# Output projection of a decoder trunk on one core: two of four column groups token-major, turned by one transpose and a trip through memory

## The chip, the cores and the metric

The kernel runs on one core of one Trainium2 chip. The metric is the device time of one execution in microseconds (us); the kernel before was run three times. The profile is of one further execution.

## The reference, cut to what matters

Two layers follow each other. The first mixes tokens (attention and retention), adds its output projection to the residual x, and runs a gated MLP; the second mixes by pooling and runs another MLP. The change lies in the output projection of the first layer and in the normalized copy of x that the MLP behind it reads:

```
def rms_norm(x, g):
    y = xf * lax.rsqrt(jnp.mean(xf * xf, axis=-1, keepdims=True) + EPS)
    return (y * g).astype(x.dtype)

# parallel_mixer: mixed is (1, 256 tokens, 2048), w_out is (2048, 2048)
    mixed = jnp.concatenate([a_out, r_out], axis=-1)
    return jnp.einsum('bse,ed->bsd', mixed, w_out)

# reference, layer 0
    x = x + parallel_mixer(...)
    h = rms_norm(x, ffn_norm[l])
    x = x + conv_ffn(h, w_up[l], conv_w[l], conv_b[l], w_down[l])
```

## The kernel before

Everything is feature-major: x is 128 partitions (features) by 16 feature tiles by S = 256 tokens. A matrix product in float32 is made of three products of rounded parts: a weight w is split in hi (rounded copy, ScalarE, L741) and lo = w - hi (VectorE, L1115), and so is the activation (first and second S columns of h, mixed and act). Products hi*hi, hi*lo and lo*hi are summed in PSUM.

Weights arrive in units of 512 x 512 (1 MB), one DMA each (L315, on SP's queue), in four slots of raw. A unit has four k-tiles (kt) of 128 rows. For each kt ScalarE writes hi[kt] as soon as TensorE has used that kt of the unit before (w_hi waits on w_used), VectorE writes lo[kt], and TensorE waits on lo_done. SP loads unit n when lo of unit n - 4 is made.

TensorE has two ways to use a unit. wide_unit (L385 to L408) keeps the weights stationary: for each kt four products hi x 512 columns (both parts of the activation, L391) and four lo x 256 columns (L395), into four PSUM banks, feature-major. token_unit (L489 to L503) keeps the activation stationary and streams the weights: for each kt six products of 512 columns (L498, L500, L501), into two banks, token-major. The down projections of both MLPs use token_unit for three of their four column groups; there VectorE turns the result with 16 transposes of 32 x 256 (turn_down, L1431) and adds it to x (add_turned).

The output projection is the stage of this case: 16 units, n = 0 to 15, four column groups of four units (n // 4). Groups alternate between banks 4 to 7 and 0 to 3. Before, all four are wide. When group g is summed, VectorE adds both halves of its banks to x in two instructions (add_mixed, L1291 and L1293), right behind its lo of unit n = 4, 8, 12. ScalarE then makes the first part of h (h_spread, L747) between its hi at n = 5, 9, 13 and one square of the group (square, L776) behind it; VectorE makes the second part of h between its lo at n = 6, 10, 14 (h_lo_group, L1150) and adds squares at n = 11, 15 (add_squares, L1125). The last group is handled inside the first units of the up projection. TensorE waits before group g for the evacuation of what the same banks held.

All orders are written out by hand; each engine's instructions run in that order, DMA issues on its own queue among them. ScalarE's queue carried few DMAs before: the gains, a strip of bias written to memory (L886) and read back (L890), and two parts of the output.

Of the kernel before, what the change touches and what calls it, by code (L numbers as in the profile page):

```python
# [23 lines left out]
ALU = mybir.AluOpType  # L24
ACT = mybir.ActivationFunctionType
AX = mybir.AxisListType
F32 = mybir.dt.float32
F32R = mybir.dt.float32r

P = 128  # L30
# [4 lines left out]
KT = 4  # L35

def trunk_kernel(nc, xT, rel_bias, norm_g, w_in, w_out, lam, subln, pool_w, pool_scale,
                 w_up, conv, w_down, bucket_onehot, rot_cos, rot_sin, decay, pool_matrix, ident_in, flip_in, outT):
    D, S = xT.shape  # L40
# [33 lines left out]
    U_OUT = U_IN + NG_IN * 4  # L74
# [6 lines left out]
    G_OUT = len(ACCS) + 1  # L81
# [26 lines left out]
    RET_START = (39, 42, 47, 49)  # L108

    scratch = nc.dram_tensor("bias_strip", (BD, SPAN), F32, kind="Internal").ap()

    TURN = 32
# [3 lines left out]
    with ctx:  # L117
# [5 lines left out]
        x = sb("x", [P, DT, S])  # L123
# [17 lines left out]
        with mixer:  # L141
            qb = [sb(f"q{i}", [P, 4, S], stack=mixer) for i in range(2)]
# [4 lines left out]
            mixed = sb("mixed", [P, DT, 2 * S], F32R, stack=mixer)  # L147
# [33 lines left out]
        ps = ctx.enter_context(nc.psum_tensor("ps", [P, 8, 512], F32))  # L181

        def sem(name):
            return ctx.enter_context(nc.semaphore(name))
# [10 lines left out]
        w_used = sem("w_used")  # L195
        evacuated = sem("evacuated")
# [40 lines left out]
        mix_hi = sem("mix_hi")  # L237
        mix_lo = sem("mix_lo")
        x_half = sem("x_half")
        x_turned = sem("x_turned")  # L240
        half_in = sem("half_in")
        half_sum = sem("half_sum")
# [19 lines left out]
        rstd_copied = sem("rstd_copied")  # L262
        out_ready = sem("out_ready")
        out_done = sem("out_done")

        rstd_b = rstd[:, 0:S]
        rstd_2 = rstd_b.unsqueeze(1).to_broadcast([P, 2, S])
# [26 lines left out]
        def wide_bank(G):  # L294

            return 4 - 4 * (G % 2)
# [83 lines left out]
        def _(pe):  # L380
            def wide_unit(n, base, bank, first, last, moving, ready=None, in_rows=None):

                for kt in range(KT):

                    pe.wait_ge(lo_done, base + KT * n + kt + 1)  # L385
                    if ready is not None:
                        ready(kt)
                    mv = moving(kt)

                    def wide(m):  # L390
                        pe.matmul(ps[:, bank + m, :], hi[:, kt, m * P:(m + 1) * P], mv, start=first and kt == 0,  # L391
                                  stop=False, skip_group_check=True)

                    def narrow(m):
                        return pe.matmul(ps[:, bank + m, S:2 * S], lo[:, kt, m * P:(m + 1) * P], mv[:, 0:S],  # L395
                                         start=False, stop=last and kt == KT - 1, skip_group_check=True)
                    if in_rows is None or kt in in_rows:
                        for row in (0, 2):
                            wide(row)
                            wide(row + 1)  # L400
                            narrow(row)
                            mm = narrow(row + 1)
                    else:
                        for m in range(4):
                            wide(m)
                            mm = narrow(m)
                    mm.then_inc(w_used, 1)

            def opening(j):

                return (0, 3) if j == 0 else ()
# [203 lines left out]
            for n in range(U_OUT):  # L615
                G, j = divmod(n, 4)
                if n in ACC_AT:
                    i = ACC_AT[n]
# [28 lines left out]
            for g in range(4):  # L647
                G = G_OUT + g
                pe.wait_ge(evacuated, G - 1)
                if g == 0:  # L650
                    pe.wait_ge(head_kept, 16)
                    pe.wait_ge(ssq_kept, 8)
                for j in range(4):
                    def mixed_tile(kt, j=j):
                        pe.wait_ge(mix_lo, (KT * j + kt) // 2 + 1)
                    wide_unit(U_OUT + 4 * g + j, 0, wide_bank(G), j == 0, j == 3, lambda kt: mixed[:, KT * j + kt, :],
                              mixed_tile if g == 0 else None, opening(j) if g else None)

            for l in range(DEPTH):
                if l == 1:  # L660
# [54 lines left out]
                for g in range(DN_GROUPS):  # L715
                    G = G_DN[l] + g
                    pe.wait_ge(evacuated, G - 1)
                    for j in range(DN_UNITS):
                        n, whole = U_DN[l] + DN_UNITS * g + j, j == DN_UNITS - 1
# [11 lines left out]
        def _(sc_e):  # L731
# [94 lines left out]
            def mixed_hi(n):  # L826
                sc_e.wait_ge(mix_f32, 2 * (n + 1))
                a_.activation(mixed[:, 2 * n:2 * n + 2, 0:S], mt[:, :, :], ACT.Copy).then_inc(mix_hi, 1)
# [74 lines left out]
                    head_root(6, 8)  # L903
            for n in range(16):
                g = n // 4 - 1
                spread = n >= 4 and n % 4 == 1
                w_hi(U_OUT + n, 0, n % 4, 16 * (R_OUT[0] + n // 4 + 1),
                     h_spread(g, 1, G_OUT + g + 1) if spread else None)
                if n == 0:
                    first_half_in(len(ACCS) - 1)  # L910
                    mixed_hi(4)
                    ret_gate(1)
                if n == 1:
                    mixed_hi(5)
                if n == 2:
                    mixed_hi(6)
                    mixed_hi(7)
                if spread:
                    square(1, g)

# [25 lines left out]
            for l in range(DEPTH):  # L946
# [105 lines left out]
                q = (l + 1) * 2 * PAIRS - 1  # L1052
# [15 lines left out]
                for g in range(1, DN_GROUPS):  # L1068
                    for j in range(DN_UNITS):
                        s = j % 4  # L1070
# [17 lines left out]
            for m in range(4):  # L1088
                t = 12 + m
# [20 lines left out]
        def _(ve):  # L1110
            def w_lo(n, base, slot, kts=range(KT), between=None):

                for kt in kts:
                    ve.wait_ge(hi_done, base + KT * n + kt + 1)
                    ve.tensor_tensor(lo[:, kt, :], raw[:, slot, kt, :], hi[:, kt, :].bitcast(F32),  # L1115
                                     ALU.subtract).then_inc(lo_done, 1)
                    if between is not None:
                        between(kt)

            def add_squares(n, g):  # L1120

                ve.wait_ge(sq_ready, 4 * n + g + 1)
                if g > 1:
                    ve.wait_ge(sq_added, SQ_BASE[n] + g - 1)
                ve.tensor_tensor(sqacc[:, :, :], sqacc[:, :, :], sqt[:, :, :], ALU.add).then_inc(sq_added, 1)  # L1125
# [20 lines left out]
            def h_lo_group(n, g, gain, ms=range(4)):  # L1146
                for m in ms:
                    t = 4 * g + m
                    ve.wait_ge(h_hi, H_BASE[n] + t + 1)
                    ve.scalar_tensor_tensor(h[:, t, S:2 * S], x[:, t, :], gains[:, gain, t:t + 1],  # L1150
                                            h[:, t, 0:S].bitcast(F32), ALU.mult, ALU.subtract).then_inc(h_lo, 1)
# [126 lines left out]
            def decay_scores(r):  # L1278
# [5 lines left out]
                ve.tensor_tensor(sc[:, 0, 0:S], ps[:, 4, 0:S], dec[:, r, :], ALU.mult).then_inc(decayed, 1)  # L1284
                ve.tensor_tensor(sc[:, 0, S:S + P], ps[:, 4, S:S + P], dec[:, r, 0:P], ALU.mult).then_inc(decayed, 1)

            def add_mixed(g):

                ve.wait_ge(w_used, KT * (U_OUT + 4 * (g + 1)))
                b, xs = wide_bank(G_OUT + g), x[:, 4 * g:4 * g + 4, :]  # L1290
                ve.tensor_tensor(xs, ps[:, b:b + 4, 0:S], xs, ALU.add).then_inc(x_half, 1)  # L1291
                ve.wait_ge(x_half, g + 1)
                ve.tensor_tensor(xs, ps[:, b:b + 4, S:2 * S], xs, ALU.add).then_inc(evacuated, 1)  # L1293

            ve.memset(ones[:, :], 1.0).then_inc(setup, 1)
# [66 lines left out]
                    norm_ret(7)  # L1362
            for n in range(16):
                g = n // 4 - 1
                spread = n >= 4 and n % 4 == 2
                w_lo(U_OUT + n, 0, n % 4, between=(lambda kt: h_lo_group(1, g, 1, [kt])) if spread else None)
                if g >= 1 and n % 4 == 3:
                    add_squares(1, g)
                if n == 0:
                    take_out(len(ACCS) - 1)  # L1370
                    mixed_lo(4)
                    mix_ret(5)
                if n == 1:
                    mixed_lo(5)
                    mix_ret(6)
                if n == 2:
                    mixed_lo(6)
                    mix_ret(7)
                    mixed_lo(7)
                if n >= 4 and n % 4 == 0:  # L1380
                    add_mixed(n // 4 - 1)

            def up_add(q, Gp):

# [54 lines left out]
            def add_down(l, g):  # L1439

                ve.wait_ge(w_used, KT * (U_DN[l] + DN_UNITS * (g + 1)))
                b, xs = wide_bank(G_DN[l] + g), x[:, 4 * g:4 * g + 4, :]
                ve.tensor_tensor(xs, ps[:, b:b + 4, 0:S], xs, ALU.add).then_inc(x_half, 1)
                ve.wait_ge(x_half, 4 + l + 1)
                ve.tensor_tensor(xs, ps[:, b:b + 4, S:2 * S], xs, ALU.add).then_inc(evacuated, 1)

            for l in range(DEPTH):
# [118 lines left out]
            for m in range(4):  # L1566
                b, xs = wide_bank(G_DN[1] + 3) + m, x[:, 12 + m, :]
                ve.wait_ge(tail_mm, m + 1)
                ve.tensor_tensor(xs, ps[:, b, 0:S], xs, ALU.add).then_inc(x_half, 1)
                ve.wait_ge(x_half, 5 + m + 1)  # L1570
                ve.tensor_tensor(xs, ps[:, b, S:2 * S], xs, ALU.add).then_inc(last_added, 1)
            ve.wait_ge(token_rms, 1)
            ve.reciprocal(rms[:, 2:4], rms[:, 0:2]).then_inc(token_rstd, 1)
# [124 lines left out]
```

## Time and profile before

| what | value |
|---|---|
| time, median of 3 runs | 1942.24 us (1942.01 to 1942.35) |
| time of the profiled execution | 1942.34 us |
| its span in the profile | 1940.2 us |
| TensorE busy | 1924.7 us, 99% |
| VectorE busy | 1428.8 us, 74% |
| ScalarE busy | 1111.5 us, 57% |
| DMA, mean | 188 GB/s |

The profile's span begins with the first instruction and ends with the last; 2.1 us of the execution lie around it. TensorE's matmuls are pipelined, so the distance from one start to the next says what one costs, not its duration.

### The profile page before, as it was taken

The numbers are of one execution on the slowest core, as the hardware profiler recorded it, in microseconds if no ns is written. First come the engines' busy times: TensorE is split into PE (matmuls) and PEld (weight loads), VectorE is DVE, ScalarE is ACT, GpSimd is POOL, SyncE is SP. The second block draws the span as 40 slices with busy tenths as digits, with TensorE's granted clock in tenths as the row PEclk, the third lists the DMA queues.
The fourth block names the chain that finished last, engine by engine and source line by source line (L and its number), as shares of the span: only waits on it lengthen the run. The fifth ranks groups of instructions, "written<-read, shape, count | busy, mean of one in ns | idle before, by whom it ended". The sixth has DMA issues, their size and how long they took to land.

```text
span 1940.2 us, 30192 instructions
## 1 busy us (share of the span) xinstructions
PE 1924.7 (99%) x10550; PEld 1665.1 (86%) x10550; DVE 1428.8 (74%) x2242; ACT 1111.5 (57%) x1845; POOL 48.7 (3%) x53
## 2 busy tenths in 40 slices
PE   8999999999999999999999999999999999999998
PEld 8888888888888888888888888888888888888887
DVE  6667786767877777777666667877777777756665
ACT  6555544656565656666544556656665566655544
POOL 0002250000000000000000000000000000000000
PEclk9999999999999999999999999999999999999999
DMA  9655555555555555555555555555555555555653
GB/s 327 196 172 160 183 164 169 190 184 190 195 183 187 193 192 182 188 194 168 200 203 191 193 173 177 192 193 183 188 194 191 182 189 195 190 170 191 214 191 108
DMA packets 205203, 364.93 MB, mean 188 GB/s; under 512 B 6563, under 2 KB 49100, under 8 KB 205132
## 3 DMA queue, kind: packets, MB, share of 16 engines
q1 hardware_dynamic: 203388, 362.34, 56.2%
q10 hardware_dynamic: 1744, 1.63, 0.3%
q8 instruction: 47, 0.77, 0.2%
q14 instruction: 24, 0.20, 0.0%
HBM read 361.83 MB, written 2.11 MB: 188 GB/s over the span
## 4 chain that ended last, share of the span: by engine, by line
PE 98%; DVE 1%; ACT 0%; DMA 0%; issue 0%; DVEq 0%; SPq 0%
PE ps L391 41%; PE ps L395 20%; PE ps L498 8%; PE ps L500 8%; PE ps L501 8%; PE ps L464 7%; PE ps L468 3%; PE ps L482 0%; PE ps L484 0%; PE ps L485 0%; DVE ssq L1245 0%; DVE lo L1115 0%; PE ps L670 0%; PE ps L672 0%; PE ps L530 0%; PE ps L583 0%
## 5 line engine op out<-in xcount | busy, mean ns | idle before, releaser
L741 ACT ACTIVATE hi<-raw 128x512 fp32r<-128x512 f32 x1352 | 844.4, 630 | 792.7 <-PE ps L395 470.0
L1115 DVE TENSOR_TENSOR lo<-raw,hi 128x512 fp32r<-128x512 f32 x1360 | 927.9, 697 | 465.1 <-ACT hi L741 459.1
L391 PE MATMUL ps<-h,hi 128*128 128x512 f32 x2816 | 958.2, 394 | 0.0
L395 PE MATMUL ps<-h,lo 128*128 128x256 f32 x2816 | 734.3, 277 | 0.0
L391 PEld LDWEIGHTS ps<-h,hi 128*128 128x128 f32 x2816 | 508.2, 188 | 98.1 <-DVE lo L1115 0.2
L395 PEld LDWEIGHTS ps<-h,lo 128*128 128x128 f32 x2816 | 529.2, 188 | 25.4
L498 PE MATMUL ps<-hi,act 128*128 128x512 f32 x528 | 205.6, 389 | 0.0
L500 PE MATMUL ps<-lo,act 128*128 128x512 f32 x528 | 205.6, 389 | 0.0
L501 PE MATMUL ps<-hi,act 128*128 128x512 f32 x528 | 205.5, 389 | 0.0
L464 PE MATMUL ps<-h,hi 128*128 128x512 f32 x576 | 183.3, 400 | 0.0
L468 PEld LDWEIGHTS ps<-h,lo 128*128 128x128 f32 x576 | 108.3, 188 | 25.4
L498 PEld LDWEIGHTS ps<-hi,act 128*128 128x128 f32 x528 | 99.1, 188 | 20.6
L501 PEld LDWEIGHTS ps<-hi,act 128*128 128x128 f32 x528 | 99.1, 188 | 20.6
L500 PEld LDWEIGHTS ps<-lo,act 128*128 128x128 f32 x528 | 99.1, 188 | 20.4
L391 PE MATMUL ps<-act,hi 128*128 128x512 f32 x336 | 116.0, 394 | 0.0
L468 PE MATMUL ps<-h,lo 128*128 128x256 f32 x576 | 113.4, 278 | 0.0
L395 PE MATMUL ps<-act,lo 128*128 128x256 f32 x336 | 91.9, 277 | 0.0
L464 PEld LDWEIGHTS ps<-h,hi 128*128 128x128 f32 x576 | 88.3, 189 | 0.5
L391 PE MATMUL ps<-mixed,hi 128*128 128x512 f32 x256 | 86.0, 395 | 0.5 <-DVE lo L1115 0.5
L391 PEld LDWEIGHTS ps<-act,hi 128*128 128x128 f32 x336 | 62.6, 188 | 14.0
L395 PE MATMUL ps<-mixed,lo 128*128 128x256 f32 x256 | 63.9, 278 | 0.0
L395 PEld LDWEIGHTS ps<-act,lo 128*128 128x128 f32 x336 | 63.1, 188 | 0.7
(191 smaller groups left out, 1493.8 us busy)
## 6 DMA issues: line engine op xcount, KB each, us to landing
raw<-in_w_up SPq DMA_DIRECT2D x176, 1024.0 KB, 5.0
raw<-in_w_down SPq DMA_DIRECT2D x88, 1024.0 KB, 5.0
raw<-in_w_in SPq DMA_DIRECT2D x54, 1024.0 KB, 5.1
raw<-in_w_out SPq DMA_DIRECT2D x16, 1024.0 KB, 5.1
raw<-in_pool_w SPq DMA_DIRECT2D x4, 1024.0 KB, 5.2
raw<-in_w_in SPq DMA_DIRECT2D x8, 256.0 KB, 4.9
x<-in_xT SPq DMA_DIRECT2D x8, 128.0 KB, 4.7
x<-in_xT SPq DMA_DIRECT2D x2, 512.0 KB, 7.8
```

The source lines that it names most:

```text
L391: pe.matmul(ps[:, bank + m, :], hi[:, kt, m * P:(m + 1) * P], mv, start=first and kt == 0, stop=False, skip_group_check=True)
L395: return pe.matmul(ps[:, bank + m, S:2 * S], lo[:, kt, m * P:(m + 1) * P], mv[:, 0:S], start=False, stop=last and kt == KT - 1, skip_group ...
L464: pe.matmul(acc[:, m, :], hi[:, kt, c], mv, start=first and kt == 0 and a == 0, stop=False, skip_group_check=True)
L468: mm = pe.matmul(acc[:, m, S:2 * S], lo[:, kt, c], mv[:, 0:S], start=False, stop=last and kt == KT - 1 and a == 1, skip_group_check=True)
L498: pe.matmul(acc[:, t, :], xh, hi[:, kt, :], start=first and kt == 0, stop=False, skip_group_check=True)
L500: pe.matmul(acc[:, t, :], xh, lo[:, kt, :], start=False, stop=False, skip_group_check=True)
L501: mm = pe.matmul(acc[:, t, :], xl, hi[:, kt, :], start=False, stop=last and kt == KT - 1, skip_group_check=True)
L741: a_.activation(hi[:, kt, :], raw[:, slot, kt, :], ACT.Copy).then_inc(hi_done, 1)
L1115: ve.tensor_tensor(lo[:, kt, :], raw[:, slot, kt, :], hi[:, kt, :].bitcast(F32), ALU.subtract).then_inc(lo_done, 1)
```

## The change

Groups 0 and 1 of the output projection are computed with token_unit, into two banks. Behind its lo of unit n = 4 (8), VectorE turns all 32 x 32 blocks of the two banks with one transpose of 128 x 1024 into turned_m, which lies where the queries lay. ScalarE's queue waits for it behind its hi of the same unit and writes the tile to memory (one DMA, 512 KB). Behind its hi of n = 5 (9) it waits for that DMA and reads the tile back with four DMAs of 128 KB, 32 partitions each, so that features are on partitions. Behind its lo of n = 6 (10) VectorE waits for all four and adds the result to x in two instructions of 128 x 512.

The first part of h and the square of groups 0 and 1 move to n = 7 and 11 on ScalarE; the second part moves to n = 8 and 12 on VectorE. The addition of squares moves from n = 11 to n = 13; group 2's square stays at n = 13. Groups 2 and 3 stay wide.

```
+    bounce = nc.dram_tensor("turned_rows", (P, 4 * S), F32, kind="Internal").ap()
+        turned_m = qb[0][:, :, :].rearrange("p q e -> p (q e)")
+        quads_m = qb[1][:, :, :].rearrange("p q e -> p (q e)")
# TensorE
+                    if g < 2:
+                        token_unit(U_OUT + 4 * g + j, ps[:, wide_bank(G):wide_bank(G) + 2, :], j == 0, j == 3, j,
+                                   mixed_tile if g == 0 else None, mixed)
+                    else:
+                        wide_unit(U_OUT + 4 * g + j, 0, wide_bank(G), j == 0, j == 3, lambda kt: mixed[:, KT * j + kt, :],
+                                  None, opening(j))
# ScalarE
-                spread = n >= 4 and n % 4 == 1
+                spread = n in (7, 11, 13)
                 w_hi(U_OUT + n, 0, n % 4, 16 * (R_OUT[0] + n // 4 + 1),
                      h_spread(g, 1, G_OUT + g + 1) if spread else None)
...
+                if n in (4, 8):
+                    sc_e.wait_ge(m_turned, g + 1)
+                    sc_e.dma_start(bounce, turned_m).then_inc(m_out, 16)
+                if n in (5, 9):
+                    sc_e.wait_ge(m_out, 16 * (g + 1))
+                    for q in range(4):
+                        there = quads_m[q * TURN:(q + 1) * TURN, :].rearrange("f (b e) -> f b e", b=4)
+                        here = bounce.rearrange("(b f) (q e) -> q f b e", b=4, q=4)[q]
+                        sc_e.dma_start(there, here).then_inc(m_in[q], 16)
# VectorE
+            def turn_mixed(g):
+                ve.wait_ge(w_used, KT * (U_OUT + 4 * (g + 1)))
+                b = wide_bank(G_OUT + g)
+                rows = ps[:, b:b + 2, :].rearrange("p t (m q f) -> p q (t m) f", m=4, q=4)
+                ve.transpose(turned_m.rearrange("p (q k s) -> p q k s", q=4, k=8), rows).then_inc(m_turned, 1)
+            def add_turned_mixed(g):
+                for q in range(4):
+                    ve.wait_ge(m_in[q], 16 * (g + 1))
+                for t in range(2):
+                    quads = quads_m.rearrange("p (b t m s) -> p t m b s", b=4, t=2, m=4)[:, t]
+                    xs = x[:, 4 * g:4 * g + 4, t * P:(t + 1) * P].rearrange("p m (b s) -> p m b s", b=4)
+                    added = ve.tensor_tensor(xs, quads, xs, ALU.add)
+                added.then_inc(evacuated, 1)
...
-                spread = n >= 4 and n % 4 == 2
-                w_lo(U_OUT + n, 0, n % 4, between=(lambda kt: h_lo_group(1, g, 1, [kt])) if spread else None)
-                if g >= 1 and n % 4 == 3:
-                    add_squares(1, g)
+                spread = n in (8, 12, 14)
+                w_lo(U_OUT + n, 0, n % 4, between=(lambda kt: h_lo_group(1, g if n == 14 else g - 1, 1, [kt])) if spread else None)
+                if n in (13, 15):
+                    add_squares(1, 1 if n == 13 else 2)
...
-                if n >= 4 and n % 4 == 0:
-                    add_mixed(n // 4 - 1)
+                if n in (6, 10):
+                    add_turned_mixed(g)
+                if n in (4, 8):
+                    turn_mixed(g)
+                if n == 12:
+                    add_mixed(2)
```

The counts of the semaphore x_half in the later stages are two lower, since two add_mixed are gone.

## Rows read from the trace of the kernel before

**Rows 1.** The page: busy time of the engines, and TensorE's clock in 40 slices.
```profile
PE 1924.7 (99%) x10550; PEld 1665.1 (86%) x10550; DVE 1428.8 (74%) x2242; ACT 1111.5 (57%) x1845; POOL 48.7 (3%) x53
PEclk9999999999999999999999999999999999999999
```

**Rows 2.** The page: the chain that ended last, shares by engine.
```profile
PE 98%; DVE 1%; ACT 0%; DMA 0%; issue 0%; DVEq 0%; SPq 0%
```

**Rows 3.** Timeline of TensorE where groups 0, 1, 2 and the up projection begin.
```profile
349.12 0.70 PE L391 MATMUL ps<-mixed,hi 128*128 128x512 f32 x2 [0.48 <-DVE lo L1115]
...
371.51 0.62 PE L391 MATMUL ps<-mixed,hi 128*128 128x512 f32 x2
...
393.71 0.62 PE L391 MATMUL ps<-mixed,hi 128*128 128x512 f32 x2
...
438.11 0.63 PE L391 MATMUL ps<-h,hi 128*128 128x512 f32 x2
```

**Rows 4.** Instructions by source line: matmuls of the down projection, with first and last start.
```profile
L498 PE MATMUL ps<-hi,act x528: 388/389/395, 927.2 to 1865.6; 128*128 128x512 f32 x176
...
L391 PE MATMUL ps<-act,hi x336: 388/394/398, 1106.7 to 1921.4; 128*128 128x512 f32 x168
```

**Rows 5.** Timeline of ScalarE, VectorE and SP behind the end of group 0.
```profile
371.70 0.63 ACT L741 ACTIVATE hi<-raw 128x512 fp32r<-128x512 f32 x1 [0.76 <-PE ps L395]
...
372.37 0.69 DVE L1115 TENSOR_TENSOR lo<-raw,hi 128x512 fp32r<-128x512 f32 x1 [0.70 <-ACT hi L741]
...
372.98 1.22 DVE L1291 TENSOR_TENSOR x<-ps,x 128x1024 f32<-128x1024 f32 x1
373.09 11.48 SPq L315 DMA_DIRECT2D raw<-in_w_out  x3
...
375.37 1.89 DVE L1115 TENSOR_TENSOR lo<-raw,hi 128x512 fp32r<-128x512 f32 x3
...
377.93 0.69 DVE L1115 TENSOR_TENSOR lo<-raw,hi 128x512 fp32r<-128x512 f32 x1 [0.67 <-ACT hi L741]
...
378.60 1.04 ACT L776 ACTIVATE sqacc<-x 128x1024 f32<-128x1024 f32 x1
...
379.55 1.14 ACT L741 ACTIVATE hi<-raw 128x512 fp32r<-128x512 f32 x2
...
380.81 0.48 DVE L1150 SCALAR_TENSOR_TENSOR h<-x,gains,h 128x256 fp32r<-128x256 f32 x1
```

**Rows 6.** The page: VectorE groups, busy us, mean ns of one.
```profile
L1431 DVE STREAM_TRANSPOSE u<-ps 32x256 f32<-32x256 f32 x96 | 42.8, 446 | 2.9
...
L1125 DVE TENSOR_TENSOR sqacc<-sqacc,sqt 128x1024 f32<-128x1024 f32 x13 | 15.9, 1219 | 2.2 <-ACT sqt L776 2.2
```

**Rows 7.** DMA issues: KB each, median us from issue to landing.
```profile
raw<-in_w_out SPq DMA_DIRECT2D x16, 1024.0 KB, 5.1
...
x<-in_xT SPq DMA_DIRECT2D x8, 128.0 KB, 4.7
x<-in_xT SPq DMA_DIRECT2D x2, 512.0 KB, 7.8
bias<-bias_strip ACTq DMA_DIRECT2D x1, 1024.0 KB, 5.6
out_T<-x SPq DMA_DIRECT2D x2, 512.0 KB, 3.9
...
dec<-in_decay SPq DMA_DIRECT2D x1, 512.0 KB, 4.5
```

**Rows 8.** Issue instructions of DMAs: two of SP at the start, one of ScalarE.
```profile
2.60 0.43 SPq L343 DMA_DIRECT2D x<-in_xT  x1
3.08 0.43 SPq L344 DMA_DIRECT2D raw<-in_w_in  x1
...
60.76 0.40 ACTq L890 DMA_DIRECT2D bias<-bias_strip  x1
```

**Rows 9.** Landing of the one weight load (L330) issued between 63 and 64 us.
```profile
DMA to landing us min/median/max: 6.2/6.2/6.2
```

More of the change, by code:

```diff
@@ L239, in trunk_kernel @@
         x_half = sem("x_half")
+        m_turned = sem("m_turned")
+        m_out = sem("m_out")
+        m_in = [sem(f"m_in{i}") for i in range(4)]
         x_turned = sem("x_turned")
@@ L655, in mixed_tile @@
                         pe.wait_ge(mix_lo, (KT * j + kt) // 2 + 1)
-                    wide_unit(U_OUT + 4 * g + j, 0, wide_bank(G), j == 0, j == 3, lambda kt: mixed[:, KT * j + kt, :],
-                              mixed_tile if g == 0 else None, opening(j) if g else None)
+                    if g < 2:
[4 more added lines that the diff above has]
+                                  None, opening(j))
             for l in range(DEPTH):
@@ L1291, in add_mixed @@
                 ve.tensor_tensor(xs, ps[:, b:b + 4, 0:S], xs, ALU.add).then_inc(x_half, 1)
-                ve.wait_ge(x_half, g + 1)
+                ve.wait_ge(x_half, g - 1)
                 ve.tensor_tensor(xs, ps[:, b:b + 4, S:2 * S], xs, ALU.add).then_inc(evacuated, 1)
@@ L1443, in add_down @@
                 ve.tensor_tensor(xs, ps[:, b:b + 4, 0:S], xs, ALU.add).then_inc(x_half, 1)
-                ve.wait_ge(x_half, 4 + l + 1)
+                ve.wait_ge(x_half, 2 + l + 1)
                 ve.tensor_tensor(xs, ps[:, b:b + 4, S:2 * S], xs, ALU.add).then_inc(evacuated, 1)
@@ L1569, in _ @@
                 ve.tensor_tensor(xs, ps[:, b, 0:S], xs, ALU.add).then_inc(x_half, 1)
-                ve.wait_ge(x_half, 5 + m + 1)
+                ve.wait_ge(x_half, 3 + m + 1)
                 ve.tensor_tensor(xs, ps[:, b, S:2 * S], xs, ALU.add).then_inc(last_added, 1)
```

## The prediction

> **What bounds the kernel now.** I read the page first: TensorE is busy 99% of the span at full clock, no other engine is above 74% [rows 1], and the chain of waits that ends last is TensorE for 98% [rows 2]. So the time is TensorE's stream of matmuls plus whatever makes it wait, and an edit on another engine is worth nothing unless weights or banks come late. The timeline of TensorE then gives the stage: group 0 of the output projection takes 371.51 - 349.12 = 22.39 us, group 1 22.20, and groups 2 and 3 together 438.11 - 393.71 = 44.40, again 22.20 each [rows 3]. At 16 k-tiles a group that is 1.40 us a k-tile in group 0 and 1.3875 behind it, for 4 x 512 + 4 x 256 = 3,072 columns.
>
> **TensorE's part.** The token-major form streams 6 x 512 = 3,072 columns too, so the change saves no column, only whatever the mixed form loses between matmuls. The down projection has this very form in this kernel: from its first L498 at 927.2 us to the first wide matmul behind it at 1106.7 [rows 4] lie 3 groups x 11 units x 4 = 132 k-tiles, 179.5 / 132 = 1.360 us each (0.227 us a matmul). A group of 16 then takes 21.76 us: group 0 gains 22.39 - 21.76 = 0.63, group 1 22.20 - 21.76 = 0.44, together 1.07 us. The stationary operand is mixed in place of act, of the same shape; bounds are the 1.07 and, if the cadence stayed that of the wide form, 0. I take 1.07, the same code at 528 instances a line.
>
> A rule of the Trainium skill speaks against even this ("TensorE: Matmul & The Clock Gate", section "Back-to-back issue gap"): an isolated warm matmul of N columns takes N / 2.4 + 2.5 ns. By that, an estimate, a k-tile costs 1.295 us token-major and 1.300 wide, and the two groups would gain 0.2 us. The rows have 1.360 and 1.3875, and the sum goes by them.
>
> **VectorE and ScalarE behind a group.** Let T be the start of group 1 on TensorE (371.51 before). Before, hi of the last k-tile of unit 4 starts at T + 0.19, its lo at T + 0.86, and VectorE's next instruction at T + 1.47 [rows 5]. From the start of a hi to the matmul that may use it are then 0.19 to 1.55, some 1.4 us with the hand-over.
>
> Removed: two add_mixed (4 instructions of 1.22 us), each of which ended 2.4 us behind its start; this was covered. Added in that place: one transpose of 128 x 1024. The trace has only 32 x 256 at 0.446 us; an elementwise instruction of 128 x 1024 takes 1.22 [rows 6]. From below 1.2; from above four times the small one, 1.8. I take 1.25, since 256 elements a partition cost the small one about what they cost an elementwise instruction: it ends at T + 2.7.
>
> ScalarE, which before went straight to unit 5, now waits until T + 2.75 and issues the write, 0.4 us [rows 8], so hi of unit 5 starts at T + 3.2, and its matmul could run at T + 4.6. TensorE comes there at T + 5.44 (4 x 1.36). Cost nothing; it would cost what a transpose above 2.1 us adds.
>
> **The write to memory: the tight place.** ScalarE waits behind hi of unit 5 for the write to land, and behind it stand four issues, then hi of unit 6. With L for issue to landing and 0.48 us from issue to issue (3.08 - 2.60, [rows 8]), hi of unit 6 starts at T + 2.8 + L + 1.9 and its matmul can run at T + 6.1 + L. TensorE is there at T + 10.88. So the write is hidden up to L = 4.8 us. In group 2 (unit 10 likewise) the transpose stands also behind one more part of h, 0.4 us ([rows 5], the 0.48 at 380.81 less overlap), and units last 5.55: 11.10 - 6.5 gives L = 4.6.
>
> What is L for 512 KB? Loads of that size landed after 3.9 us (output, at the end) and 4.5 (decay table, amid other loads), 7.8 in the crowd of the first 10 us; 1 MB alone takes 5.1 [rows 7]. The write is not alone: a weight load goes out at T + 1.58 ([rows 5], 373.09), 1.2 us before it. The one case of two such transfers side by side is the bias table, 1 MB at 5.6 from ScalarE's queue [rows 7], with a weight load issued 2.3 us later that took 6.2 in place of 5.1 [rows 9]: sharing adds 0.5 to 1.1. So L lies between 3.9 and 5.6, with 7.8 as the far end. I take 4.5, the same size amid other loads: no stall, with 0.1 to 0.3 us to spare. At 5.6 TensorE waits 0.8 + 1.0 = 1.8 us; at 7.8, 3.0 + 3.2 = 6.2. The weight loads, if delayed by 1 us, have room: SP issues them at the last lo four units ahead, and they are wanted three units (16 us) later.
>
> The Trainium skill ("DMA: Bandwidth & Descriptors", section "Anatomy of one DMA") gives about 2.0 us plus bytes / 436 GB/s, fitted on another engine's path, and blames most of the fixed part on the write's receipt, memory being the slowest target. By it the write would take 3.2 us; 1 MB would take 4.4 by it, and the row has 5.1. This trip pays that fixed part twice, once each way.
>
> **Reading back and adding.** The four reads are issued from T + 7.3 (L = 4.5), the last at T + 8.75. A load of 128 KB lands 4.7 us after issue in the crowd of the start [rows 7], so at T + 13.4 at the latest. VectorE stands ready at T + 10.88 + 1.47 = T + 12.35; two additions of 128 x 512 take 0.69 each (the size of a lo, [rows 5]), some 1.4, and lo of unit 7 another 0.7. TensorE wants unit 7 at T + 16.32, so the additions may start at T + 14.1: hidden, 0.7 us to spare. A landing of 1 us more costs 0.3. Group 2 waits for this evacuation at T + 21.76, 6 us later: no cost.
>
> **The steps moved.** h of group 0 on VectorE beside n = 8 is the 0.4 already counted. Beside n = 12 it delays add_mixed(2) by 0.4: before, lo of unit 5 began at 375.37 and was done at 376.06, for a matmul at 371.51 + 5.55 = 377.06, so 1.0 us to spare becomes 0.6. At n = 13 ScalarE's square of group 2 now waits for add_squares, which VectorE makes behind its last lo of that unit: by the pattern of rows 5, that lo ends at 377.93 + 0.69 = 378.6, the addition at 379.8, where the square before began at 378.60. So hi of unit 14 starts at 379.55 + 1.25 = 380.8 and is usable at 382.2, for a matmul at 371.51 + 11.10 = 382.6. Hidden by 0.4; if both delays add up, by nothing, at a price of 0.1. Squares' and h's last users come in the up projection, where group 3 arrives last as before. All costs nothing.
>
> **Sum.** 1940.2 - 1.07 + 0 = 1939.1 us of span, plus the 2.1 around it: 1941.3; the profiled execution is 0.1 above the median, so 1941.2 us.
>
> **Rivals.** A difference under 0.2% (3.9 us) is about what a measurement of this kernel can tell from no change.
> 1. The forecast: the cadence of the down projection, transfers hidden or nearly so (up to 0.4 us of stall in all). 1941.1 to 1941.7. Chance 0.58.
> 2. The write lands late, L between 4.9 and 6.5: ScalarE's hi of units 6 and 10 are late. For it: both queues share the engines, the weight load has just left. Against: 3.9 and 4.5 in the rows. At 5.6: 1941.2 + 1.8 = 1943.0. Chance 0.22.
> 3. No gain: TensorE streams 3,072 columns either way and mixed behaves as in the wide form (the page's rule above comes to nearly this). 1942.0 to 1942.3. Against: the down projection. Chance 0.12.
> 4. Slower past the bound: the trip through memory crowded as at the start. It needs 3.9 + 1.1 = 5.0 us of stall in two groups, that is 2.5 each, L above 7.2; at 7.8 it is 1941.2 + 6.2 = 1947.4. Against: the stage moves 1 MB every 5.5 us, where the start was crowded by a dozen transfers. Chance 0.05.
> 5. Something gained elsewhere, since banks come free sooner: no wait for banks is in the chain, so under 0.5 us. Chance 0.03, and hardly past 3.9 us.
>
> The range 1940.8 to 1943.2 holds rival 1, 3 and most of 2 (up to L = 5.7), some 0.85. Chances: faster by over 0.2% 0.01, within 0.94, slower 0.05.
>
> **What the profile after would show.** Group 0 and group 1 at 21.8 us each between first matmuls; L498 on mixed at 0.227 us a step. One STREAM_TRANSPOSE of 128 x 1024 near 1.25 us, twice. The write landing 4.5 us after issue, the reads under 5. ScalarE idle before its hi of units 6 and 10 by the transfer, TensorE not. Wrong if TensorE shows a gap at the first matmul of units 6, 7, 10, 11 or 14 (a late transfer, a late addition, or the square), or if the transpose takes over 2 us.

## The result, and the profile after

The changed kernel takes 1945.32 us (median of 20 runs, 1943.39 to 1946.25), the kernel before 1942.36 in the same comparison (20 runs, 1941.77 to 1943.55): a ratio of 1.0014 with a 95% interval of 1.0007 to 1.0020. It is 3.0 us slower, where 1.1 us less was forecast and 1943.2 was the upper end of the range. The profiled execution took 1945.25 us.

The page of the changed kernel, the lines that answer to [rows 1] and [rows 2]:

```profile
PE 1926.3 (99%) x10486; PEld 1663.2 (86%) x10486; DVE 1427.9 (73%) x2244; ACT 1110.0 (57%) x1845; POOL 48.7 (3%) x53
PEclk9999999999999999999999999999999999999999
...
PE 98%; DVE 1%; DMA 0%; ACT 0%; ACTq 0%; POOLq 0%; issue 0%; SPq 0%; DVEq 0%
```

On this page almost nothing has moved: TensorE is still busy 99% and the clock looks full in every slice of 48 us. In the chain only the order of the shares near 0% has changed, and two queues, ScalarE's (ACTq) one of them, are new in it. The loss is in the timeline of TensorE (changed kernel; start, length, line, and in brackets the idle time before and who ended it), which answers to [rows 3]:

```profile
348.39 0.47 PE L505 MATMUL ps<-hi,mixed 128*128 128x512 f32 x1 [0.48 <-DVE lo L1135]
...
370.27 0.39 PE L505 MATMUL ps<-hi,mixed 128*128 128x512 f32 x1
...
380.92 0.39 PE L508 MATMUL ps<-hi,mixed 128*128 128x512 f32 x1
383.15 0.50 PE L505 MATMUL ps<-hi,mixed 128*128 128x512 f32 x1 [1.84 <-DVE lo L1135]
...
384.00 0.63 PE L505 MATMUL ps<-hi,mixed 128*128 128x512 f32 x1
384.42 0.63 PE L507 MATMUL ps<-lo,mixed 128*128 128x512 f32 x1
384.85 0.63 PE L508 MATMUL ps<-hi,mixed 128*128 128x512 f32 x1
...
395.78 0.62 PE L398 MATMUL ps<-mixed,hi 128*128 128x512 f32 x2
...
407.13 0.50 PE L398 MATMUL ps<-mixed,hi 128*128 128x512 f32 x1
...
418.53 0.64 PE L398 MATMUL ps<-mixed,hi 128*128 128x512 f32 x2
...
440.80 0.40 PE L398 MATMUL ps<-h,hi 128*128 128x512 f32 x1
```

Read it from start to start. Group 0 takes 370.27 - 348.39 = 21.88 us, 0.5 less than before: the gain is there. Unit 6 was due 0.227 behind 380.92, at 381.15, and came at 383.15, 2.0 us late. Behind it matmuls stand 0.427 us apart where 0.227 is normal. Group 1 so takes 25.51 us in place of 21.76. Group 2 begins unit 10 0.25 us late (407.13; due 395.78 + 11.10 = 406.88) and takes 22.75. The windows of the same trace (busy us of each engine, then granted clock, DMA share, GB/s) show what happened in between:

```profile
375.00:381.10 6.10, 6.10 (x28) 4.88 (x26) 1.72 (x3) 0.81 (x2) 0.00 (x0) 1.00 0.90 292
381.10:383.15 2.05, 0.21 (x1) 0.00 (x1) 0.74 (x2) 1.41 (x3) 0.00 (x0) 1.00 0.79 263
383.15:387.30 4.15, 4.15 (x11) 3.33 (x12) 2.46 (x5) 1.42 (x3) 0.00 (x0) 0.59 0.60 135
387.30:395.00 7.70, 7.70 (x35) 6.34 (x35) 4.77 (x8) 5.87 (x11) 0.00 (x0) 1.00 0.55 183
```

TensorE was idle for 2 us, and then the granted clock was 0.59 for 4.15 us, that is 1.2 GHz for most of it and 2.4 again from 387.3. Eleven starts that take 2.49 us at full clock took 4.2 (383.15 to 387.36): 1.7 us more on top of the 2.0.

Who was late, in the timeline of ScalarE and its queue (changed kernel):

```profile
373.02 0.34 ACTq L931 DMA_DIRECT2D turned_rows<-q  x1
373.46 1.72 ACT L752 ACTIVATE hi<-raw 128x512 fp32r<-128x512 f32 x3 [2.36 <-PE ps L508]
375.91 0.63 ACT L752 ACTIVATE hi<-raw 128x512 fp32r<-128x512 f32 x1 [0.73 <-PE ps L508]
379.08 2.56 ACTq L937 DMA_DIRECT2D q<-turned_rows  x4
381.74 2.19 ACT L752 ACTIVATE hi<-raw 128x512 fp32r<-128x512 f32 x4 [5.20 <-PE ps L508]
...
398.92 0.35 ACTq L931 DMA_DIRECT2D turned_rows<-q  x1
...
403.85 1.76 ACTq L937 DMA_DIRECT2D q<-turned_rows  x4
```

and in the timeline of VectorE, the transpose of group 0 and its additions:

```profile
371.74 1.24 DVE L1312 STREAM_TRANSPOSE q<-ps 128x1024 f32<-128x1024 f32 x1
...
386.60 1.29 DVE L1321 TENSOR_TENSOR x<-q,x 128x512 f32<-128x512 f32 x2 [1.70 <-DMA q<-turned_rows]
```

With T = 370.27, the write goes out at T + 2.75, as forecast. The four reads behind its landing are issued from 379.08, 6.06 us later (4.5 was assumed), and take 2.56 us to issue (1.9 was assumed). hi of unit 6 starts at 381.74 and its matmul at 383.15, 1.41 later. The bracket of ScalarE names TensorE as releaser ("5.20 <-PE") because it counts from the end of ScalarE's last work and the buffer's release came before; the issues on the queue right ahead of it are what held it. In group 2 the write takes 403.85 - 398.92 = 4.9 us and unit 10 is 0.25 late. The additions of group 0 wait for the reads until 386.60, T + 16.3, past the T + 14.1 that would have been in time; TensorE was behind by then, so nobody saw it.

The stage from group 0 to the up projection takes 440.80 - 348.39 = 92.41 us, before 88.99 [rows 3]: 3.4 more. The stage began 0.7 us earlier in this execution (TensorE had come to full clock at 8.4 us, at 10.1 in the profile before) and what follows took 0.2 longer, which gives the 2.9 of the spans (1943.1 and 1940.2).

### The profile page after: what moved, and what is told of

It is laid out like the page before. It is cut to its first block, busy times and chain, and to the rows that moved or that the text cites. A ratio compares the mean times of both kernels' runs of the same rounds, so it can differ in the third digit from the quotient of the medians.

```text
span 1943.1 us, 30080 instructions
## 1 busy us (share of the span) xinstructions
PE 1926.3 (99%) x10486; PEld 1663.2 (86%) x10486; DVE 1427.9 (73%) x2244; ACT 1110.0 (57%) x1845; POOL 48.7 (3%) x53
## 4 chain that ended last, share of the span: by engine, by line
PE 98%; DVE 1%; DMA 0%; ACT 0%; ACTq 0%; POOLq 0%; issue 0%; SPq 0%; DVEq 0%
PE ps L398 39%; PE ps L402 19%; PE ps L505 9%; PE ps L508 9%; PE ps L507 8%; PE ps L471 7%; PE ps L475 3%; PE ps L489 0%; PE ps L491 0%; PE ps L492 0%; DVE lo L1135 0%; DMA turned_rows<-q 0%; DVE ssq L1265 0%; ACT hi L752 0%; PE ps L681 0%; PE ps L683 0%
## 5 line engine op out<-in xcount | busy, mean ns | idle before, releaser
L505 PE MATMUL ps<-hi,h 128*128 128x512 f32 x160 | 63.3, 395 | 0.3 <-DVE lo L1135 0.3
L508 PE MATMUL ps<-hi,h 128*128 128x512 f32 x160 | 62.3, 390 | 0.0
```

The lines of the kernel that those rows point to most:

```text
L505: pe.matmul(acc[:, t, :], xh, hi[:, kt, :], start=first and kt == 0, stop=False, skip_group_check=True)
L508: mm = pe.matmul(acc[:, t, :], xl, hi[:, kt, :], start=False, stop=last and kt == KT - 1, skip_group_check=True)
```

## The experiments

Three explanations are tested. A: the write lands late, ScalarE behind it makes hi of unit 6 late, and TensorE's wait is paid nearly twice because the clock falls. B: the reads and additions are late. C: the token-major form on mixed, the transpose or the moved steps cost the time. Times are medians in us, each beside the kernel before on the same chip; "stage" is from the first matmul of group 0 to the first of the up projection in the profiled execution.

| run | time | before | ratio, 95% interval | stage |
|---|---|---|---|---|
| changed kernel | 1945.32 | 1942.36 | 1.0014 (1.0007 to 1.0020) | 92.4 |
| e1_no_trip | 1941.65 | 1942.72 | 0.9996 (0.9987 to 1.0005) | 88.0 |
| e7_h_moved | 1942.61 | 1942.72 | 0.9999 (0.9990 to 1.0009) | 89.0 |
| e5_dose2 | 1943.43 | 1942.72 | 1.0004 (0.9995 to 1.0014) | 89.9 |
| e11_dose3 | 1945.05 | 1942.38 | 1.0013 (1.0004 to 1.0023) | 90.9 |
| e6_dose4 | 1947.36 | 1942.72 | 1.0024 (1.0014 to 1.0033) | 93.6 |
| e2_sp_queue | 1946.03 | 1942.39 | 1.0017 (1.0007 to 1.0026) | 92.8 |
| e4_act_late | 1944.89 | 1942.39 | 1.0014 (1.0004 to 1.0023) | 90.7 |
| e8_load_held | 1944.67 | 1942.39 | 1.0011 (1.0002 to 1.0021) | 90.7 |
| e3_sp_late | 1941.51 | 1942.39 | 0.9996 (0.9987 to 1.0005) | 88.0 |
| e12_sp_late_again | 1941.39 | 1942.38 | 0.9995 (0.9986 to 1.0004) | 88.0 |
| e10_reads_later | 1941.37 | 1942.38 | 0.9995 (0.9986 to 1.0004) | 88.1 |

**Without the trip** (e1_no_trip). The run leaves out the write and the reads, so its x is in the wrong order; TensorE's work is the same.

```
-                if n in (4, 8):
-                    sc_e.wait_ge(m_turned, g + 1)
-                    sc_e.dma_start(bounce, turned_m).then_inc(m_out, 16)
-                if n in (5, 9):
-                    sc_e.wait_ge(m_out, 16 * (g + 1))
...
             def add_turned_mixed(g):
-                for q in range(4):
-                    ve.wait_ge(m_in[q], 16 * (g + 1))
+                ve.wait_ge(m_turned, g + 1)
                 for t in range(2):
-                    quads = quads_m...
+                    quads = turned_m...
```

> The changed kernel without the trip through memory: no write, no reads, no waits for them; the two additions take the turned tile as it lies, so features of x are in wrong places and the output is not the reference's. Theory A (late transfer: the write holds ScalarE, unit 6 comes 2 us late, and TensorE's clock falls behind the wait): both go, 1942.4 - 1.1 = 1941.3 us, TensorE without a gap in the stage. Rival B (it is the reads and the additions that come late, not the write): the same here, told apart by the runs with the additions one unit later. Rival C (the token-major form on mixed, the transpose or the moved steps cost it): 1943 us or more, with the gap still there.

1941.65 us, and no gap in the stage, which takes 437.72 - 349.69 = 88.03 us, 0.96 less than before. So the token-major form, the transpose and the moved steps give the forecast's gain, and all of the loss belongs to the trip. C falls.

**Only the steps of h moved** (e7_h_moved), in the kernel before:

```
-                spread = n >= 4 and n % 4 == 1
+                spread = n in (7, 11, 13)
...
-                spread = n >= 4 and n % 4 == 2
+                spread = n in (8, 12, 14)
-                if g >= 1 and n % 4 == 3:
+                if n in (13, 15):
```

> The kernel before, all four groups wide and added as before, with only the steps of h and of the squares moved to the units of the changed kernel. A and B: within 0.3 us of 1942.4, no gap on TensorE at units 8, 13 or 14. C in the form of the moved steps: 1 us or more above, with a gap at unit 14.

1942.61 us against 1942.72, a stage of 89.03, no gap. The moved steps cost nothing here either.

**What a wait of TensorE costs** (e5_dose2, e11_dose3, e6_dose4). In the kernel before, k = 2, 3 or 4 copies without any use hold up ScalarE, so that hi of unit 6 and TensorE come late by a chosen amount:

```
                 if spread:
                     square(1, g)
+                if n == 5:
+                    sc_e.wait_ge(table_in, 16 * N_TABLE)
+                    for i in range(k):
+                        a_.activation(yv[:, :, :], pool_m[:, :, 0:S], ACT.Copy).then_inc(dose, 1)
+                        sc_e.wait_ge(dose, i + 1)
```

> The kernel before with two copies of 128x1024 (table to a buffer not yet in use, about 1.2 us each with the wait behind it) on ScalarE behind its square at n = 5. hi of unit 6 then starts 2.4 us later, of which 1.6 are spare: TensorE waits 0.8 us once. If a wait costs only itself: 1943.2 us. If the clock falls even behind so short a wait: about 1944 or more.

> The same with four copies, 4.9 us: TensorE waits 3.3 us once. If a wait costs only itself: 1945.7 us. A says that the wait is paid about 2 us more through the clock: 1947.7 us, with matmuls of 512 columns 0.427 us apart for some 4 us behind the gap.

> The kernel before with three copies on ScalarE behind n = 5. By the two doses measured (gap 0.5 us and 2.7 us) TensorE waits 1.6 us once. If the clock falls behind it as behind 2.7: 1942.4 + 1.6 + 2 = 1946.0; if not: 1944.0 to 1944.5.

Two copies: unit 6 came 0.5 us late (383.71, due 0.12 behind 383.08), time + 0.7. Four: 2.7 us late where 3.3 was expected, time + 4.6, as A said (1947.7 expected, 1947.36 measured). TensorE's timeline in the run with four, start to start of a wide and a narrow matmul first 0.35 us, then 0.64:

```profile
383.08 0.27 PE L396 MATMUL ps<-mixed,lo 128*128 128x256 f32 x1
385.89 0.50 PE L392 MATMUL ps<-mixed,hi 128*128 128x512 f32 x1 [2.53 <-DVE lo L1121]
...
386.69 0.61 PE L392 MATMUL ps<-mixed,hi 128*128 128x512 f32 x1
387.10 0.42 PE L396 MATMUL ps<-mixed,lo 128*128 128x256 f32 x1
387.31 0.63 PE L392 MATMUL ps<-mixed,hi 128*128 128x512 f32 x1
387.74 0.41 PE L396 MATMUL ps<-mixed,lo 128*128 128x256 f32 x1
```

and the windows of the same run, from the late matmul on:

```profile
385.89:386.70 0.81, 0.81 (x5) 0.72 (x6) 0.81 (x2) 0.78 (x2) 0.00 (x0) 1.00 0.00 0
386.70:389.90 3.20, 3.20 (x13) 2.72 (x12) 3.13 (x7) 0.63 (x1) 0.00 (x0) 0.50 0.00 0
389.90:400.00 10.10, 10.10 (x58) 8.76 (x58) 4.47 (x7) 4.43 (x7) 0.00 (x0) 0.99 0.60 208
```

So 1.2 GHz for a little over 3.2 us, beginning 0.8 us behind the gap, with no other change in the kernel: the clock's part belongs to the idle time, not to the token-major form. With three copies unit 6 of the profiled execution came 1.6 us late (383.80, due 382.20; the bracket counts the idle time, 1.44) with full clock behind it (windows, the second fence):

```profile
383.80 0.50 PE L392 MATMUL ps<-mixed,hi 128*128 128x512 f32 x1 [1.44 <-DVE lo L1121]
```

```profile
383.80:390.00 6.20, 6.20 (x35) 5.40 (x36) 5.24 (x10) 2.93 (x6) 0.00 (x0) 1.00 0.30 96
```

That execution took 1943.8 us, the shortest of its ten; the median is 1945.05. Whether the clock fell in the others is open, since only one of them was traced. The 1.3 us between do not show it: the stage of the traced execution began at 348.67, 1.0 us before those of the runs with two and four copies (349.66 and 349.65), so most of the difference can lie ahead of the stage. The expectation (1944.0 to 1944.5 with full clock, 1946.0 otherwise) was met by neither branch.

**The same transfers on SP's queue** (e2_sp_queue), all else as in the changed kernel:

```
 # SP, behind the load of unit n
+                if n in (8, 12):
+                    sp.wait_ge(m_turned, n // 4 - 1)
+                    sp.dma_start(bounce, turned_m).then_inc(m_out, 16)
+                if n in (9, 13):
+                    sp.wait_ge(m_out, 16 * (n // 4 - 1))
+                    for q in range(4):
+                        ... the four reads, on sp
 # ScalarE: the same lines removed
```

> The changed kernel with the write and the four reads issued on SP's queue (write behind the load of unit 8 or 12, reads behind that of 9 or 13); ScalarE issues and waits for nothing; additions still at n = 6 and 10. A: unit 6 is in time; the reads are issued from T + 9 to T + 11 (T: start of group 1 on TensorE) and land 5.4 to 6.4 us later, T + 16 to 17, so VectorE's additions end at T + 17.5 and unit 7, due at T + 16.3, waits 2 us, and the clock falls behind it: 1944 to 1946, the gap moved from unit 6 to unit 7. If the write alone is the cause (narrow form of A): 1941.3.

1946.03 us. The gap has moved from unit 6 to unit 7, as A said (this run's timeline of TensorE, then of VectorE):

```profile
388.03 0.39 PE L517 MATMUL ps<-hi,mixed 128*128 128x512 f32 x1
391.06 0.80 PE L514 MATMUL ps<-hi,mixed 128*128 128x512 f32 x1 [2.64 <-DVE lo L1135]
391.66 0.63 PE L516 MATMUL ps<-lo,mixed 128*128 128x512 f32 x1
```

```profile
389.11 1.29 DVE L1321 TENSOR_TENSOR x<-q,x 128x512 f32<-128x512 f32 x2 [4.74 <-DMA q<-turned_rows]
```

ScalarE was free in time, unit 6 had no gap, and VectorE now stood 4.7 us before its additions for reads that took 6.3 to 7.2 us to land. Unit 7 came 2.8 us late with half clock behind (its unit took 6.89 us in place of 5.44). So in the changed kernel a second late step stood behind the first and was hidden by it: B is true too, as the next one in the row. The narrow form of A (the write alone) falls.

**Only the additions and h one unit later** (e4_act_late), transfers on ScalarE's queue as in the changed kernel:

```
 # VectorE
-                if n in (6, 10):
+                if n in (7, 11):
                     add_turned_mixed(g)
 # h and square of groups 0, 1, 2: ScalarE n = 8, 12, 14; VectorE n = 9, 13, 15
```

> The changed kernel with its transfers on ScalarE's queue as they are, and only the additions and h one unit later as in the run before. A: the first gap stands, unit 6 is 1 to 2 us late and the clock falls: 1944 to 1946. B: the gap goes, 1941.3.

1944.89 us: the gap at unit 6 stands (383.34, 1.1 us late in the profiled execution, with full clock behind it) and unit 10 is 1.0 late. B alone falls. The part of A's expectation that the clock falls was not seen in this execution; the stage is 2.7 us longer than without the trip by 2.15 us of waits and a slower pace behind them (last section).

**Both together** (e3_sp_late and e12_sp_late_again): SP's queue and the additions one unit later (the two diffs above).

> As the run before (SP's queue), and additions one unit later (n = 7, 11), h and square of groups 0, 1, 2 on ScalarE at n = 8, 12, 14, on VectorE at n = 9, 13, 15. A: every landing has 2 us or more to spare, no gap: 1941.3 us, faster than both. C: still above 1942.4.

> The version with the transfers on SP's queue and the additions one unit later, once more and on the same chip as the two others: 1941.5 us, 0.9 below the kernel before.

1941.51 and 1941.39 us, no gap at any unit, stage 88.0. In group 0 of the first run the write took 5.9 us and the reads 5.9 to 6.6, about as long as in the changed kernel, and it no longer matters: VectorE reaches its additions without a wait at 388.62. The last read had landed at 386.97, so 1.6 us were to spare and not the 2 expected. In the second run reads took up to 7.8 us and still came in time.

**Only later reads and later additions, all on ScalarE's queue** (e10_reads_later):

```
 # against the run with the additions one unit later
-                if n in (5, 9):
+                if n in (6, 10):
                     sc_e.wait_ge(m_out, 16 * (g + 1))
```

> The changed kernel with its transfers on ScalarE's queue, the four reads issued one unit later (behind hi of units 6 and 10) and the additions and h later as in the run with the ACT queue and late additions. The write still lands 6 us after its issue, T + 9, but hi of unit 6 no longer stands behind it, and the issues (2.6 us) end near T + 14.3, hi of unit 7 is usable at T + 15.7, due at T + 16.3. A: no gap at unit 6; the reads land near T + 19, the additions end at T + 20.6, unit 8 is due at T + 21.8: no gap or one under 0.5 us, 1941.4 to 1942 us. If it is not the position of the wait but the traffic: 1944 or more.

1941.37 us, no gap, with one line changed from a kernel of 1944.89. The write still took 6.1 us; hi of unit 6 simply stands ahead of the wait now. What cost the time was the place of the wait in ScalarE's order; the write itself is no faster. In group 0 the first three reads, issued 4 us or more behind a weight load, landed after 4.1 to 4.4 us, and the fourth, issued together with the next load, after 6.3. VectorE waited for them before its additions (2.6 us over both groups), which cost TensorE nothing.

**Why the write takes 6 us: the weight load beside it held back** (e8_load_held).

```
 # SP, ahead of the load of unit n
+                if n in (8, 12):
+                    sp.wait_ge(m_out, 16 * (n // 4 - 1))
                 unit(wout, ...)
```

> The changed kernel with one thing more: SP holds the weight load of unit 8 (12) until the write has landed. If sharing the engines with that load is what makes the write slow: landing falls from 6.0 to 4.0 us, ScalarE is free in time, unit 6 is not late; the reads still land some 5.5 us behind their issues, at T + 14.3, so at most 0.3 us at unit 7: 1941.3 to 1942. If the write is slow by itself (receipt of a write to memory): landing stays near 6 and the time near 1945.

The write landed after 2.6 us in both groups, where 4.0 was expected (rows of this run's trace, the write of group 0, and then the third and fourth read):

```profile
L933 ACTq DMA_DIRECT2D turned_rows<-q x1: 345/345/345, 374.3 to 374.3; - x1
...
DMA to landing us min/median/max: 2.6/2.6/2.6
```

```profile
DMA to landing us min/median/max: 7.2/7.6/8.0
```

Alone it needs 2.6 us, behind a load of 1 MB issued 1.2 us ahead 6.0. So it is the load that made it slow, not the write to memory as such. The packets tell more: the first fence is the view of the DMA queues in the first 3.2 us behind the write's issue in the changed kernel (373.02 to 376.20), the second the same in this run until the write has landed (374.25 to 376.88). q1 is SP's queue, q10 ScalarE's; the numbers are packets, MB, and share of the engines' time.

```profile
q1 hardware_dynamic: 392, 0.80, 83.0%
```

```profile
q10 hardware_dynamic: 144, 0.52, 49.1%
```

With the load ahead, not one packet of the write ran in those 3.2 us, and it landed at 379.06, 1.25 us behind the load (377.81). So it went in all twelve cases, two groups in each of the six runs that have a write behind a load: the write landed 1.23 to 1.26 us behind the load, on ScalarE's queue (changed kernel, e4_act_late, e10_reads_later) and on SP's (e2_sp_queue, e3_sp_late, e12_sp_late_again) alike. Group 2 of the changed kernel has 4.9 us because its load had been issued 1.56 us ahead and took 5.2. The load took 6.0 us in group 0, in place of 5.1 in the kernel before. The Trainium skill ("DMA: Bandwidth & Descriptors", section "Queues, rings and completion order") says that each DMA engine takes turns between the queues with work; these rows do not show such turns, neither in the first 3.2 us nor as a difference between one queue and two. Why the write's packets begin so late is open.

The held load then ran beside the reads, which took up to 8.7 us (5.5 were expected), so the additions came late (units 7 and 11 by 0.7 and 1.5 us) and the time was 1944.67: the part of the expectation that put it at 1941.3 to 1942 was wrong. Moving a collision is not removing it.

## Why the prediction was wrong, point by point

- **TensorE's cadence.** Right. 1.360 us a k-tile was forecast from the down projection, and the stage is 0.84 to 0.99 us shorter in the four runs without a gap (1.07 forecast; 0.1 of the difference is the start of group 0). The formula for an isolated matmul that the prediction set beside its sum gave 0.2 us; it does not hold for this stream.
- **The transpose.** Right: 1.24 us against 1.25, and the write's issue at T + 2.75 to the hundredth.
- **The write's landing.** This is the step that failed: "I take 4.5, the same size amid other loads". It took 6.0 us in group 0 and 4.9 in group 2, outside the bounds 3.9 to 5.6 in the first. The runs show in its place that the write lands about 1.25 us behind the weight load issued ahead of it, and 2.6 us after its issue when there is none. By this even a load of the usual 5.1 us, issued at T + 1.58, gives L = 1.58 + 5.1 + 1.25 - 2.8 = 5.1, past the 4.8 that were hidden; the load took 6.0. The bias table was the right row to look at, but from its wrong side ("sharing adds 0.5 to 1.1"): there the table was ahead and the weight load, 2.3 us behind, was the one that stood where the write stands here, and it needed 6.2. The row of 3.9 was misread too: it is the median of two writes of the output, not of loads. They took 3.3 and 4.5 us beside other parts of the output, and the first two parts, of 256 KB each, took 2.2 and 2.3, so the range hid how fast such a write is alone.
- **The four issues.** Taken as 4 x 0.48 = 1.9 us, they took 2.6 in group 0 and 1.8 in group 2; single ones 0.31 to 0.92 us.
- **The price of a stall.** Taken as its own length. With the measured landing and issues the forecast's own sum gives 1.3 + 0.7 = 2.0 us late at unit 6, which is what the trace has; the clock then added 1.7 us that the prediction had no term for. In group 2 a wait of 0.25 was followed by 0.3 us more in the stage. Together 2.25 us of waits cost 4.4 us (stage 92.41 against 88.03 without the trip).
- **Reads and additions.** "At T + 13.4 at the latest" was wrong too: the last landed near T + 16.3, 5.3 to 6.4 us behind its issue. It cost nothing in the changed kernel only because TensorE was late already; on SP's queue it cost the whole gap again.
- **The moved steps.** Right: no cost (1942.61 against 1942.72), and square and additions of group 2 left unit 14 in time.
- **Rivals.** Rival 2 was the mechanism, with 0.22, at 1943.0 for a landing of 5.6. Its price was too low by the clock and by the issues. The range had room for 2.0 us of waits and none for the clock. The chance of 0.94 for "within 0.2%" agrees with the 0.14% measured, but the sign was missed.

Two orders of the same instructions that keep both waits out of the way (SP's queue with later additions, or ScalarE's queue with reads and additions one unit later) give 0.9 to 1.0 us less than the kernel before in three comparisons, each with an interval that still holds no change; the stage in the profiles, 88.0 and 88.1 us against 89.0, says it more sharply. So nearly all of the gain that was forecast exists.

## What to carry to other kernels

Where an engine in strict order waits for a transfer, ask what stands behind the wait and when that is due, and move the wait behind the work that is due first: here one unit was worth 3.5 us. Price the landing from the transfer that was issued just ahead (here 1.25 us behind its landing for 512 KB), not from a typical row of the same size, and then look for the next late step behind it. In the profiled executions waits of TensorE of 2.0 and 2.7 us cost 1.7 us more through its clock and one of 2.8 us 1.5, so the price of a wait is not its length.

## What was not expected of the hardware

- The clock behind a wait. In the profiled executions TensorE's waits of 2.0, 2.7 and 2.8 us were followed by matmuls at 1.2 GHz for about 3 us; behind waits of 0.5, 0.7, 1.0, 1.1, 1.5 and 1.6 us the granted clock stayed at 1.00. Each is one execution; whether a wait of the same length always does the same was not measured. The Trainium skill ("TensorE: Matmul & The Clock Gate", section "HAM oscillation — how this bites in real kernels") tells of waits for a transfer of about 3 to 5 us that make the clock fall and the next matmuls run slow. The traces agree in kind, but here 2.0 to 2.8 us were enough.
- Behind a short wait, with the granted clock at 1.00, the next two or three wide units took longer: 5.75, 5.65 and 5.62 us in place of 5.55 in the run with two copies, and much the same with three copies and in group 2 of the changed kernel, 0.3 to 0.4 us a time. Token-major units did so for one unit only (5.57 in e4_act_late and 5.62 in e8_load_held, then 5.44 as always). Why is open; no run was made for it.
- A write of 512 KB to memory landed in 2.6 us when no other transfer was in flight, and about 1.25 us behind a weight load issued 1.2 to 1.6 us ahead of it, whichever of the two queues it was on.
- The issue of one small DMA on ScalarE's queue took 0.31 to 0.92 us, and four in a row 1.8 to 2.6 us, in the same kernel.
